# One side operation in place of three with each step of the values and gates, in the first pair of heads of both retention layers

## The reference, cut to what matters

```
h = rms_norm(x, pre_norm[layer])
proj = h @ w_in[layer]                       # 1024 x 8192
c_b, c_c, c_x, c_z, r_q, r_k, r_v, r_z = split(proj)
y_conv = c_b * causal_depthwise_conv(c_c * c_x, conv_w) * silu(c_z)
ret = retention(rotary(r_q), rotary(r_k), r_v)
ret = ret * rsqrt(mean(ret*ret) + eps)
y_ret = ret * silu(r_z)
out = concat(y_conv, y_ret) @ w_out[layer]
x = x + rms_norm(out, post_norm[layer])
```

## Time and profile before

| | |
|---|---|
| device time, median of 3 runs | 1863.78 us (1862.0 to 1865.23) |
| profiled execution, its own time | 1860.51 us |
| its span | 1858.7 us |
| mean granted TensorE clock | 0.996 of full |
| PE busy | 1828.9 us, 98% |
| DVE busy | 1320.4 us, 71% |
| ACT busy | 897.2 us, 48% |

### The profile page before, as it was taken

One profiled execution on the slowest core, in us unless ns is written; L12 is line 12 of the kernel. 1 busy time (PEld: TensorE's weight loads), 2 busy tenths in 40 slices (PEclk: granted clock), 3 DMA queues, 4 the chain that ended last, 5 costly groups with the idle time before them and its releaser, 6 DMA issues.

```text
span 1858.7 us, 32873 instructions
## 1 busy us (share of the span) xinstructions
PE 1828.9 (98%) x13810; PEld 1735.4 (93%) x13810; DVE 1320.4 (71%) x2366; ACT 897.2 (48%) x1722; POOL 112.0 (6%) x95
## 2 busy tenths in 40 slices
PE   8999999999999999999999999999998999999998
PEld 7999999877899998999899999999898999999987
DVE  5888897577656773566688686969367868686844
ACT  6222333577734432343446565656346555555632
POOL 0000000000000000000012111111000111111000
PEclk9999999999999999999999999999998999999999
DMA  5322222201132223222257575755332566666431
GB/s 182 101 85 78 88 92 91 69 24 39 53 97 92 86 83 105 92 83 87 83 133 161 132 154 137 148 137 125 114 91 75 122 140 146 140 147 140 110 124 69
DMA packets 219971, 197.75 MB, mean 106 GB/s; under 512 B 5559, under 2 KB 216304, under 8 KB 219823
## 3 DMA queue, kind: packets, MB, share of 16 engines
q1 hardware_dynamic: 174398, 173.09, 29.7%
q0 software_dynamic: 45408, 22.55, 9.9%
q10 hardware_dynamic: 16, 0.00, 0.0%
HBM read 193.53 MB, written 2.10 MB: 105 GB/s over the span
## 4 chain that ended last, share of the span: by engine, by line
PE 94%; DVE 4%; ACT 1%; issue 1%; DMA 0%; DVEq 0%; SPq 0%; ACTq 0%
PE ps L195 68%; PE ps L199 23%; PE ps L204 3%; DVE wlo L210 1%; DVE tlo L210 0%; DVE h L218 0%; DVE sw L210 0%; DVE mxl L210 0%; ACT nhi L207 0%; DVE kr L210 0%; DMA xt<-in_x_dram 0%; DVE tf L218 0%; ACT p L207 0%; DVE qr L210 0%; DVE na L210 0%
## 5 line engine op out<-in xcount | busy, mean ns | idle before, releaser
L210 DVE TENSOR_TENSOR wlo<-raw,whi 128x1024 fp32r<-128x1024 f32 (+1 forms) x351 | 415.9, 1192 | 307.7 <-ACT whi L207 306.8
L207 ACT ACTIVATE whi<-raw 128x1024 fp32r<-128x1024 f32 (+1 forms) x351 | 360.0, 1029 | 308.3 <-PE ps L195 274.1
L195 PE MATMUL ps<-nhi,whi 128*128 128x256 f32 (+3 forms) x1840 | 406.9, 289 | 3.6 <-DVE nlo L210 2.0
L195 PE MATMUL ps<-nhi,wlo 128*128 128x256 f32 (+3 forms) x1840 | 403.2, 287 | 0.0
L195 PE MATMUL ps<-nlo,whi 128*128 128x256 f32 (+3 forms) x1712 | 366.1, 287 | 0.0
L195 PEld LDWEIGHTS ps<-nhi,whi 128*128 128x128 f32 x1840 | 297.2, 190 | 7.6 <-DVE nlo L210 2.3
L195 PEld LDWEIGHTS ps<-nhi,wlo 128*128 128x128 f32 x1840 | 296.3, 190 | 2.1
L195 PEld LDWEIGHTS ps<-nlo,whi 128*128 128x128 f32 x1712 | 271.8, 190 | 1.9
L199 PE MATMUL ps<-thi,whi 128*128 128x256 f32 x688 | 197.8, 287 | 0.2
L199 PE MATMUL ps<-thi,wlo 128*128 128x256 f32 x688 | 194.8, 283 | 0.0
L199 PE MATMUL ps<-tlo,whi 128*128 128x256 f32 x688 | 194.6, 283 | 0.0
(11 more groups left out here) (312 smaller groups left out, 3314.6 us busy)
## 6 DMA issues: line engine op xcount, KB each, us to landing
raw<-in_w_in_dram SPq DMA_DIRECT2D x90, 1024.0 KB, 5.5
raw<-in_w_up_dram SPq DMA_DIRECT2D x22, 1024.0 KB, 5.1
raw<-in_w_out_dram SPq DMA_DIRECT2D x20, 1024.0 KB, 5.0
s1t<-in_w_in_dram SPq DMA_DIRECT2D x43, 256.0 KB, 3.3
s1t<-in_w_in_dram POOLq DMA_DIRECT2D x43, 256.0 KB, 6.6
raw<-in_w_in_dram POOLq DMA_DIRECT2D x43, 256.0 KB, 4.7
raw<-in_w_down_dram SPq DMA_DIRECT2D x8, 768.0 KB, 4.3
raw<-in_w_down_dram SPq DMA_DIRECT2D x8, 640.0 KB, 4.0
```

Of the source, the lines that this page charges most:

```text
L195: return pe.put(after, lambda e: e.matmul(o, w, m, start=start, stop=stop_), mark)
L207: return ac.put(after, lambda e: e.activation(o, i, func, **kw))
L210: return dv.put(after, lambda e: e.tensor_tensor(o, a, b, op))
```

## The change

Three places. In pair 0 of each layer, each of the 16 steps of v and z queues one side operation in place of three. The list is no longer emptied behind z in pair 0, so what is left goes with the steps of x. In layer 1 it is emptied ahead of the c tile.

```
-                                tick(3)
+                                tick(3 if p else 1)
...
-                    loose_run(len(loose))
+                    loose_run(len(loose) if p else 0)
...
-                            loose_run(len(loose) if kind == "z" else 0)
+                            loose_run(len(loose) if kind == "z" or (l, p, kind) == (1, 0, "c") else 0)
```

## The result

| | before | changed |
|---|---|---|
| device time, median | 1861.83 us (6 runs, 1861.29 to 1865.23) | 1855.51 us (6 runs, 1854.97 to 1856.29) |
| profiled execution, its span | 1858.7 us | 1853.5 us |
| mean granted clock in it | 0.996 | 0.997 |

The ratio is 0.9962, 95% interval 0.9949 to 0.9975: faster by 0.25 to 0.51%. The forecast was 1856.0 us, within 1853.0 to 1859.5. The three more runs of the kernel before lie lower than the three shown ahead, so the gain is 6.3 us by the medians, where 7.8 was forecast. The interval of the ratio is 4.7 to 9.5 us, so the two cannot be told apart by these runs.

What follows compares the result with a forecast made beforehand. TensorE was taken as the bound, busy 1828.9 of 1858.7 us, so only its waits or slow running could be won. 1.2 + 6.7 - 0.1 = 7.8 us off 1863.78 gave 1856.0 us, range 1853.0 to 1859.5.

Steps and rivals of the forecast that it cites:

- Layer 0: Pair 0: four of eight `final_norm` operations move behind the weight slot, and TensorE's wait for it goes: 1.2 us gained.
- Layer 1 up to z's second half: Pair 0: the slot's low part is done sooner; z's second half starts at 1419.5 in place of 1426.01, without a wait.
- Where the wait goes: Layer 1: the statistics are late next; TensorE idles 2.1 us ahead of x, which starts at 1427.3; 6.7 us gained.
- The operations beside x: Layer 1: nine token sums left behind `vsc` fit beside x; least margins 0.9 and 1.1 us; 0.1 us for small frictions.
- The drain: Behind ScalarE's table load in layer 1: none taken; with about 1380 ns the transposes would wait 0.5 us, the sum 7.3.
- The sum: Whole kernel: 1.2 + 6.7 - 0.1 = 7.8 us gained, 1856.0 us against the median of the runs shown.
- The clock: Behind the new 2.1 us wait ahead of x in layer 1: TensorE's clock stays full, no fall taken.
- the rival: The clock falls after the new wait ahead of x: price up to 2.3 us, gain 5.5, 1858.3 us; chance 0.15.
- The price of the old low clock: Layer 1, behind the old 6.44 us slot wait: the first six matmul groups took 2.3 us more at half clock.

Runs made afterwards that it cites:

- second set: The changed kernel run again unedited, on another chip: 1855.36 us (7 runs), ratio 0.9969 to the kernel before.
- e1: Against the kernel before, one side operation per step in layer 0's first pair alone, layer 1 as before: 1860.77 us, ratio 0.9992.
- e3: The changed kernel, but with two side operations per step in layer 1's first pair in place of one: 1860.04 us, ratio 0.9987.
- e2: Against the kernel before, one side operation per step in layer 1's first pair alone, layer 0 as before: 1859.60 us, ratio 0.9982.
- e4: The changed kernel, but layer 1 queues nothing from the eighth step to z's end, then three with each step of x: 1856.04 us, ratio 0.9961.
- e9: The kernel before, filled with fifty unread matmuls behind the statistics' columns in layer 1, for times only: 1861.64 us, ratio 0.9994.
- e7: The changed kernel, but in layer 1, pair 0 the first turning back of the heads' results comes one step later: 1854.87 us, ratio 0.9966.
- e8: The changed kernel with statistics at the tenth step, `dg` behind `vsc`, and the turning back one step later: 1851.25 us, ratio 0.9949.

## Why the prediction was right, and where not

**Layer 0**, 1.2 us: 1.25 in the trace, 1.4 with the edit alone. The slot's wait went, nothing behind it appeared, and the wait ahead of the eight stayed at 1.06.

**Layer 1 up to z's second half**: it starts 0.85 us behind the columns, without a wait, as replayed (0.8 to 0.9). Up to here the replay can be read with an offset of 1.12 us, by which the columns come later than 1418.62.

**Where the wait goes**: replayed `nx` 1422.8, measured 1422.8 (1423.91 less 1.12); `vtk` 1426.7 against 1426.9; x 1427.3 against 1427.6; the wait 2.1 against 2.17. The 0.2 us are `dg`, 1.08 us in place of 0.88. The two edits that shorten the chain show that it sets this wait.

**The operations beside x**: `rbc` done at 1435.3 for 1435.1, `r` after 0.57 us of idleness, the third `tlo` at 1437.2 for 1436.9, and no wait in c, as forecast. The margin of about a microsecond is real too: with four operations more beside x and x 2.3 us sooner, c waits 0.98 us, which by an estimate (2.3 less 0.98) puts the margin at 1.3 us where the replay had 1.1.

**The drain** behind the table load, for which the Trainium skill (ScalarE: Activation LUTs, What ACT_TABLE_LOAD costs) gives about 1380 ns: the load ends at 1431.49 and `sz` starts at 1431.51 in the trace after. No run here shows the drain, and the transposes did not wait.

**The sum**, 7.8 us: 7.7 in the local time. By the medians it is 6.3 and, in the second set, 6.4 us, inside an interval that holds 7.8 as well. The mechanism was right, term by term, in the execution traced. That the forecast of 1856.0 us comes within 0.5 us of the median owes something to luck: it started from the median of three runs, 1863.78, which the six runs put 1.95 us lower, and this error and the 1.5 us of missing gain nearly cancel.

**The clock** is the step that failed, though the traced execution hides it. The prediction took one row, a wait of 1.69 us with a clock of 1.00 behind it, as the end of the scale at which the clock stays, and gave a fall 0.15. Over all 14 profiled executions:

| wait of TensorE | fell to 0.50 behind it |
|---|---|
| 6.4 us, for the slot (the kernel before, e1) | 2 of 2 |
| 2.6 us, for the slot (e3) | 1 of 1 |
| 1.9 to 2.3 us, ahead of x | 2 of 5 (e2, e3) |
| 1.76 to 1.99 us, for `sz` | 6 of 6 |
| 1.69 to 1.71 us, for `sz` | 2 of 5 (e1, e3) |
| 0.39 to 1.21 us, in layer 1: ahead of x, for `sz`, for `mxf` behind it, for the slots in e4 and e9 | 0 of 12 |

The length alone does not decide: 2.06, 2.15 and 2.17 us ahead of x had no fall, and 1.93 had one. The changed kernel, profiled twice, had it both ways behind `sz`. So a row with the full clock behind a wait of this length says little of the next execution, and each such wait has a price that is paid in some executions only: 1.3 to 1.5 us behind `sz`, 1.5 to 1.7 ahead of x, where the rival had up to 2.3. At 376 us, where no edit reaches, the clock fell in 8 of 14, at 1.5 or 2.8 us. The Trainium skill (TensorE: Matmul & The Clock Gate, Part 1) calls the number of slow matmuls at a kernel's start variable from run to run; these traces show the like in the middle of a kernel.

How much of the 1.5 us between the forecast gain and the medians such falls explain is not settled. Each run's mean granted clock is on record, to a thousandth, though not where it fell. In the changed kernel's second set the time goes with it, from 1858.15 us at 0.995 to 1854.18 at 0.999, about 1 us for each thousandth; all six runs of the first set stand at 0.997, so a typical run of it is 1 to 2 us above one without falls (an estimate from these two sets; the executions traced without any of these falls, of e7 and e8, stand at 0.999). But the kernel before varies as well, from 0.994 to 0.998, and on the chip of the second set the fastest runs of the two kernels, 1860.56 and 1854.18 us, lie 6.4 apart too. So the spread goes with the clock, but the falls are not shown to make up the missing 1.5 us.

**The price of the old low clock**, named as 2.3 us, was right as a length, but 1.3 of it counted; the filled kernel shows that. The sum did not need it, since it went from x's start to x's start.

## What to carry to other kernels

When side work is put in steps beside the main products, ask of each queued operation what stands behind it in the same list. Replay the new order with the old rows and name what is late next, here a chain of 4 us of small operations ahead of the next tile's bank; two moved calls then won another 2 us of local time. Where a kernel has waits of one to three microseconds in dense matmuls, look at the granted clock behind them in several executions before giving a fall a chance, and compare two kernels between fixed points of their traces as well as by their medians.

## What was not expected of the hardware

The clock can be at the lower level behind a wait as short as 1.70 us, and behind a wait of about 1.7 us it was in some executions of one program and not in others (1.76 and 1.71 us in the changed kernel). Behind waits of up to 1.21 us in dense matmuls no fall was seen. In the sparse part at 370 to 384 us, where TensorE has small matmuls and no wait over 0.9 us, the clock went to the lower level in 8 of 14 executions, which made that part up to 2.8 us longer.
